# DeltaNet decays masked by VectorE's subtraction instead of by a select on GpSimd

## The reference

```
def _chunk_gated_delta(q, k, v, g, beta, s0, need_out):
    ...
    g = jnp.cumsum(g.reshape(B, H, N, C), -1)
    incl = jnp.tril(jnp.ones((C, C), bool))
    strict = jnp.tril(jnp.ones((C, C), bool), -1)
    decay = jnp.where(incl, jnp.exp(jnp.where(incl, g[..., :, None] - g[..., None, :], 0.0)), 0.0)
    kb = k * beta[..., None]
    a = jnp.where(strict, jnp.einsum('bhnid,bhnjd->bhnij', kb, k) * decay, 0.0)
    t_inv = lax.linalg.triangular_solve(eye + a, ...)
    ...
    attn = jnp.where(incl, jnp.einsum('bhnid,bhnjd->bhnij', q, k) * decay, 0.0)
```

## Time and profile before

| | us |
|---|---|
| median of 3 executions | 2766.04 |
| lowest, highest | 2765.73, 2767.35 |
| the profiled execution: its time | 2767.35 |
| the profiled execution: span of its instructions | 2765.6 |

### The profile page before, as it was taken

How to read it: one execution, slowest core, us unless ns; L and a number is a source line. 1 busy time by engine, 2 the same in 40 slices (tenths; PEclk the granted TensorE clock), 3 DMA queues, 4 the chain that set the end, 5 groups by cost and what they waited for, 6 DMA issues and landing times. The chain is left out here.

```text
span 2765.6 us, 135980 instructions
## 1 busy us (share of the span) xinstructions
PE 2504.3 (91%) x57273; PEld 2179.1 (79%) x57273; DVE 1772.1 (64%) x2056; ACT 1557.9 (56%) x1972; POOL 817.6 (30%) x647
## 2 busy tenths in 40 slices
PE   8999997999999875999999999999988999999993
PEld 2444555899997544998989898889988999999993
DVE  2434896666665776254363655877777877778883
ACT  3521552544555435164464665777777766677873
POOL 1201102667672113122222222322223332323321
PEclk9999998999999986999999999999999999999996
DMA  9501001000002228265383856988889978889976
GB/s 366 215 26 36 3 1 31 25 31 23 23 30 89 92 77 342 72 209 206 114 303 106 311 189 236 375 314 323 312 318 323 331 271 289 312 293 343 352 256 202
DMA packets 124489, 536.93 MB, mean 194 GB/s; under 512 B 12540, under 2 KB 13552, under 8 KB 91616
## 3 DMA queue, kind: packets, MB, share of 16 engines
q1 hardware_dynamic: 107120, 481.80, 46.4%
q0 software_dynamic: 14464, 47.79, 7.7%
q10 hardware_dynamic: 2832, 6.37, 0.6%
HBM read 496.99 MB, written 38.92 MB: 194 GB/s over the span
## 5 line engine op out<-in xcount | busy, mean ns | idle before, releaser
L2394 PE MATMUL ps<-qkv,weights 128*128 128x64 f16 x10496 | 938.2, 193 | 66.1 <-issue 34.2
L2394 PEld LDWEIGHTS ps<-qkv,weights 128*128 128x128 f16 x10496 | 921.3, 98 | 82.0 <-issue 49.4
L2395 PE MATMUL ps<-qkv,weights 128*128 128x64 f16 x10496 | 937.1, 193 | 3.1 <-issue 3.1
L2396 PE MATMUL ps<-qkv,weights 128*128 128x64 f16 x10496 | 937.0, 193 | 0.6 <-issue 0.6
L2396 PEld LDWEIGHTS ps<-qkv,weights 128*128 128x128 f16 x10496 | 922.9, 98 | 2.5 <-issue 2.5
L2395 PEld LDWEIGHTS ps<-qkv,weights 128*128 128x128 f16 x10496 | 922.9, 98 | 0.8 <-issue 0.8
L1842 DVE SCALAR_TENSOR_TENSOR weights<-hT,weights 128x2048 f16<-128x2048 f16 (+1 forms) x256 | 585.5, 2339 | 161.3 <-ACT weights L1270 132.1
L1270 ACT ACTIVATE weights<-hT 128x2048 f16 (+1 forms) x256 | 527.0, 2100 | 81.2 <-DMA hT<-in_w_gu_dram 61.4
L2411 PE MATMUL ps<-qkv,weights 128*128 128x64 f16 x5248 | 471.9, 193 | 24.5 <-DVE weights L1847 22.2
L2411 PEld LDWEIGHTS ps<-qkv,weights 128*128 128x128 f16 x5248 | 461.1, 98 | 32.3 <-DVE weights L1847 27.8
L2412 PE MATMUL ps<-qkv,weights 128*128 128x64 f16 x5248 | 471.6, 193 | 0.0
(11 more groups left out here) (422 smaller groups left out, 4381.3 us busy)
## 6 DMA issues: line engine op xcount, KB each, us to landing
hT<-in_w_gu_dram SPq DMA_DIRECT2D x256, 1024.0 KB, 8.9
qkv<-in_w_down_dram SPq DMA_DIRECT2D x128, 1024.0 KB, 6.0
weights<-in_w_ada_dram SPq DMA_DIRECT2D x12, 2048.0 KB, 16.3
qkv<-in_w_in_dram SPq DMA_DIRECT2D x4, 2048.0 KB, 7.9
hT<-decay_rows SPq DMA_DIRECT2D x20, 256.0 KB, 3.2
hT<-beta_rows SPq DMA_DIRECT2D x20, 256.0 KB, 3.2
qkv<-in_x_dram ACTq DMA_DIRECT2D x8, 512.0 KB, 6.5
weights<-in_w_in_dram SPq DMA_DIRECT2D x2, 2048.0 KB, 14.4
```

Source lines behind the costliest of these rows:

```text
L2394: pe.matmul(dst, ghi[k][:, b, c], xT[:, 0, k, :], start=first, stop=False, skip_group_check=True)
L2395: pe.matmul(dst, ghi[k][:, b, c], xT[:, 1, k, :], start=False, stop=False, skip_group_check=True)
L2396: last = pe.matmul(dst, glo[k][:, b, c], xT[:, 0, k, :], start=False, stop=end, skip_group_check=True)
```

## The change

The four per-head DVE instructions of `decays` become `scalar_tensor_tensor`: the difference as before, but the minimum is taken with `zmask` of that direction instead of with 0. Where the decays count this is the minimum with 0 as before; elsewhere it is -1e30, and the exponential on ACT makes it 0. GpSimd's `select` is gone with its event; `e_D` now comes from ACT. Apart from that, the semaphore between L1935 and L1948 becomes one of its own; it counted on in another one before.

```diff
-        e_x = Event(sem("decay_exponentials_ready"), 2)
-        e_D = Event(sem("decays_masked"), 2)
+        e_D = Event(sem("decay_exponentials_ready"), 2)
...
-            def select(s, ahead):
-                for r in range(DIRS):
-                    e_x.now(pool, s, r, ahead)
-                    pool.sem_inc(s_idle, 1)
-                    pool.affine_select(out=dn[r]["decay"], in_=dn[r]["decay"], compare_op=ALU.is_ge, fill=0.0, base=0,
-                                       pattern=[[0, H], [1 - 2 * r, P]], channel_multiplier=2 * r - 1).then_inc(e_D.sem, 1)
...
             def first():
...
-                select(0, 0)
                 first_blocks(0, 0)
...
                     stage_chunk(s, next_out, 1)
-                    select(s, 1)
                     first_blocks(s, 1)
...
-                act.activation(d["decay"], d["decay"], ACT.Exp).then_inc(e_x.sem, 1)
+                act.activation(d["decay"], d["decay"], ACT.Exp).then_inc(e_D.sem, 1)
...
-                    last = dve.tensor_scalar(d["decay"][:, h, :], d["eg"][:, h, :], gs[:, r, h:h + 1], 0.0, ALU.subtract,
-                                             ALU.min)
+                    last = dve.scalar_tensor_tensor(d["decay"][:, h, :], d["eg"][:, h, :], gs[:, r, h:h + 1],
+                                                    zmask[:, r, :], ALU.subtract, ALU.min)
...
-                dve.tensor_tensor(scaled[:, n % 2, :], acc[:, n, :], g2row, ALU.mult).then_inc(s_ssq, 1)
+                dve.tensor_tensor(scaled[:, n % 2, :], acc[:, n, :], g2row, ALU.mult).then_inc(s_scl, 1)
...
-                dve.wait_ge(s_ssq, NA + n + 1)
+                dve.wait_ge(s_scl, n + 1)
```

More of the change, by code:

```diff
@@ L341, in hybrid_block @@
         s_modA = sem("beta_decay_weights_then_scale_then_decays_ready")
-        s_ssq = sem("x_squares_summed_then_expert_sums_scaled")
+        s_ssq = sem("x_squares_summed")
         s_xn = sem("x_normed")
@@ L460, in hybrid_block @@
         s_out = sem("results_stored")
+        s_scl = sem("expert_sum_scaled")
         def chunk_of(s, r, out, ahead=0):
@@ L778, in _ @@
             e_st.ahead(pool)
-            e_D.ahead(pool)
             e_B.ahead(pool)
@@ L1112, in _ @@
                     act.activation(square[:, j % 2, 0:n], qkvT[:, ct, t0:t0 + n], ACT.Square).then_inc(s_sq, 1)
-            for e in (e_x, e_KA, e_Pc, e_Xc, e_Th, e_F, e_vn):
+            for e in (e_D, e_KA, e_Pc, e_Xc, e_Th, e_F, e_vn):
                 e.ahead(act)
```

## The result

| | us, median (lowest to highest) | executions |
|---|---|---|
| before, measured again beside it | 2767.35 (2765.73 to 2771.79) | 5 |
| changed | 2786.2 (2784.68 to 2793.94) | 5 |

The ratio is 1.0076, 95% interval 1.0060 to 1.0091: slower, where 2767.8 us and "the same" were forecast, and outside the range. The profiled execution took 2787.3 us, its span is 2785.6, 20.0 more than before.

The account below looks back on a forecast made before the run. The inverse's six-level chain through PE, ACT and DVE was taken to bound the scan. Terms 1.9 - 0.1 + 0 = 1.8 us on the median 2766.04 gave 2767.8 us; own range 2764.8 to 2771.5, overall 2763 to 2773.

Parts of the forecast that it names:

- The blocked run: Direction 0's four decay instructions on DVE beside GpSimd's blocks in the loop: 3.26 us, forecast 0.24 longer a run.
- PE's wait: PE waiting for DVE's L1621 at level 4: 2.32 us, forecast to grow by 0.24 to 2.5 to 2.6.
- the select: GpSimd's select of 0.70 and 0.64 us in a loop step, ahead of a 2.64 us wait; removal forecast worth 0.
- A: Rival: GpSimd doesn't block the new form, runs take 1.1 us; 2739, or 2749 if the clock falls stay; 6 in 100.
- C: Rival: the longer form loses its turn between GpSimd blocks, 0.55 us a run, 2772.2 us in total; 3 in 100.
- D: Rival: the select was in the way after all, its removal winning 3 us in all, 2763 us; 4 in 100.
- rival B: PE restarts later at L2194 in the loop, long half-clock falls return, 3.0 us each, 2773.8 with two; 9 in 100.
- four equal steps of 40.97: Loop steps from 648.28 us on, taken to show a settled step; steps of 40.9 to 41.2 us were forecast.
- one long fall more or less: Allowance for the loop's half-clock stretches: one long instead of short, 3.0 us either way in the total.
- The forecast's own range: The forecast's total with its terms' bounds and 3.0 us for the clock: 2764.8 to 2771.5 us; 78 in 100.
- Direction 1's 0.26 us: Direction 1's unblocked decays in a loop step: 0.26 us longer, held covered by L1621's 0.17 us wait for ACT; priced 0.

Follow-up runs that it names:

- direction 1's form alone: Kernel before, select kept, with the new form of the decays' DVE instructions for direction 1 only: 2775.18 us, ratio 1.0016.
- the changed kernel's second profile: The changed kernel run once more, unaltered, beside the kernel before on another chip: 2789.6 us, ratio 1.0073.
- five linked memsets: Kernel before plus five small DVE memsets, each waited for by DVE itself, behind direction 0's decays in the seven loop steps: 2794.45 us, ratio 1.0086.
- direction 0 alone: Kernel before, select kept, with the new form of the decays' DVE instructions for direction 0 only: 2788.22 us, ratio 1.0070.
- the small dose: Kernel before plus four small memsets of a dead tile behind direction 0's decays in the seven loop steps: 2782.62 us, ratio 0.9986.

## Why the prediction was wrong

**What held.** The blocked run grew by 0.24 us in each of the seven loop steps (3.50), PE's wait with it (22.4 us in all), the select was worth nothing, and rivals A, C and D did not occur. In steps that kept their kind of fall the price was near, too: with a long fall 44.20 us against 43.97, 0.23 more, where PE restarts about as far into the fall (0.49 and 0.46 us in), and with a short fall 41.13 against 40.97, 0.16 more (0.24 and 0.05 us in).

**What failed: the clock.** The prediction argued against rival B that a PE that comes later into a fall does less work at half clock, which pays back part of the 0.24, and that four equal steps of 40.97 show a settled state. Both are borne out: a step with a short fall grew by 0.16 us where its work grew by 0.47. The conclusion, that one long fall more or less bounds the harm, isn't. What counts is where the restart lies in the fall. The start of a fall comes from a stretch of 1.00 us with its mean clock c: as the clock is 1.00 ahead of the start and 0.50 behind it, the start lies 2 x (1 - c) us ahead of the stretch's end, good to about 0.01 us. Before, in the settled state, and in the changed kernel:

```profile
692.50:693.50 1.00, 0.61 (x12) 0.61 (x13) 0.66 (x3) 0.18 (x1) 1.00 (x3) 0.67 0.54 178
815.30:816.30 1.00, 0.51 (x10) 0.51 (x11) 0.76 (x3) 0.08 (x1) 1.00 (x3) 0.71 0.58 162
```
```profile
699.20:700.20 1.00, 0.43 (x9) 0.43 (x10) 0.84 (x3) 0.00 (x0) 1.00 (x3) 0.63 0.53 186
743.50:744.50 1.00, 0.44 (x9) 0.44 (x10) 0.83 (x3) 0.01 (x1) 1.00 (x3) 0.66 0.55 195
784.50:785.50 1.00, 0.31 (x6) 0.32 (x7) 0.96 (x3) 0.00 (x0) 1.00 (x3) 0.64 0.81 199
```

Before, the fall starts at 693.50 - 0.66 = 692.84 and PE restarts at 692.89, 0.05 us into it: short. Three steps later it starts at 815.72 and PE restarts at 815.79, 0.07 in. In the long fall before these, which starts at 607.50 (mean clock 0.75 from 607.00 to 608.00), PE restarted at 607.96, 0.46 in. Changed, they start at 699.46, 743.82 and 784.78, and PE restarts 0.31 us into the first (long), 0.24 into the second (short) and 0.41 into the third (long). With direction 1's form alone the two starts are

```profile
614.00:615.00 1.00, 0.48 (x10) 0.48 (x11) 0.79 (x3) 0.05 (x1) 1.00 (x3) 0.65 0.55 188
655.00:656.00 1.00, 0.46 (x9) 0.47 (x10) 0.81 (x3) 0.03 (x1) 1.00 (x3) 0.63 0.65 135
```

614.30 and 655.26: 0.22 us in (short) and 0.28 in (long). In all eight profiles with such falls (seven kernels, the changed one twice), from the second loop step on, 48 restarts in all, those up to 0.24 us in have a short fall and those from 0.26 on a long one; the 0.26 is the last step of the changed kernel's second profile. That is a rule read from these profiles; no run moves the restart alone and leaves all else.

The drift does the rest. After a short fall the next one starts 40.96 us later (784.78 - 743.82). Before, a step with a short fall was 40.96 to 40.98, so the restart stayed almost where it was for five steps, 0.05 to 0.08 us in. Changed, the step is 41.13 (785.19 - 744.06), and the restart moves 0.17 us further in: from 0.24 to 0.41, over the border. After a long fall the next one starts 44.36 us later (743.82 - 699.46) while the step is 44.29 (744.06 - 699.77), so the restart moves back by only 0.07; the two long steps before it moved it back by somewhat more, and three of them were needed to get one short. That is the sequence seen: long three times, short, long twice. It gives direction 1 alone too: its drift of some 0.06 a step (41.02 less 40.96) needs several steps to reach the border, so most falls stay short, and it measured 0.16% and not 0.7%. With five linked memsets all restarts come over 1.1 us in, by the same working, and the steps reach 44.35, so none comes back.

So the step of the prediction that failed is the one on the clock: it held that the settled step would stay settled with 0.24 more in it (40.9 to 41.2 us), bounded the harm by one long fall, and gave rival B 9 in 100. The runs show that the step stays settled only while it is as long as the falls are apart, 40.96 us, and that the change makes it 0.16 longer, which adds up from step to step until the fall turns long. Part of that stood in the trace before: the spacing, and one restart 0.46 us in with a long fall beside five within 0.08 with short ones. How far the border is did not. The forecast's own range took one long fall, and they were four and a middle one.

**A term mis-sized.** Direction 1's 0.26 us was priced at 0 from a step at half clock. At full clock it costs 0.23 a step (0.47 less direction 0's 0.24). In the changed kernel no loop step is free of a fall, so of it little was paid here (direction 0 alone took 260.65 us, both 260.80), but it sets what is left when the clock is held: 2.87 us over six steps. The forecast's own range is also added up 0.2 us short at its top (2766.04 + 2.7 + 3.0 is 2771.7), which changes nothing.

**What stays open.** Why the border lies between 0.24 and 0.26 us is not shown. Nor is where the middle fall in the first loop step comes from: it came with direction 1 alone too, where PE waited the old 2.32 us (restart at 571.88), so it doesn't need the longer wait; it may have to do with when the loop starts, which no run varies alone. Nor is it shown what makes the other 3 us, which arise behind the scan, among the experts. Rows of one of the last stage's lines in two profiles of the changed kernel, the first and the later one:

```profile
L2411 PE MATMUL ps<-ident,qkv x664: 270/273/421, 1132.2 to 2749.8; 128*64 128x128 f32 x166
```
```profile
L2411 PE MATMUL ps<-ident,qkv x664: 271/273/422, 1130.8 to 2746.0; 128*64 128x128 f32 x166
```

The stretch between the two starts took 1617.6 us and 1615.2, so more than 2 us there come and go without a change of the kernel.

## What to carry to other kernels

Where the clock falls once in each step of a loop, a step time that repeats to the hundredth need not be slack: compare the step with the spacing of the falls and ask where a small, lasting addition drifts to, before pricing it at its own length. Read cover from a step at full clock, since idle time seen at half clock is gone when the clock is back. And when one engine's short run takes nearly four times its free length beside another's long row of instructions, try holding the other back for a microsecond: this gave 1.2% here, and taking the same work to a third engine 0.45%.

## What the runs showed of the hardware that was not expected

- Where PE came back from its wait went with how long the half clock lasted, 3.4 or 10 us, to within 0.06 us: restarts at 0.22 and 0.28 us into a fall, in one kernel (direction 1 alone) and one step apart, behind the same wait of 2.32.
- A loop with short falls took up a very small addition, not a larger one: with PE's wait 0.05 us longer (the small dose) the steps settled at 40.95 to 40.99, while direction 1's new form gave 41.02 step after step and the restart wandered, 0.01, 0.08 and 0.15 us into the fall.
- Fourteen matmuls that nothing reads, in PE's wait, left no fall in the loop and made the kernel before 0.8% faster; the changed one with them was faster than the kernel before without (0.9941).
- Being blocked doesn't hide a longer instruction: the new form, 0.066 us longer each, lengthens a run of four that GpSimd blocks by 0.24 us and a free one by 0.26.
- Small memsets in a row start 13 ns apart (three in 0.09 us), but with a wait on each they cost 0.14 us apiece (five in 0.71).
